# Five seams of a hybrid attention and DeltaNet block reordered, and three of seven weight low parts moved to GpSimd

## What is computed

```
proj = x @ w_in                       # 1024 x 4872, split into the parts below
A = banded_sink_attention(rope(q), rope(k), v)          # 8 heads, window of 128 rows
B = gated_delta_rule(conv+silu(q, k, v), beta, decay)   # 4 heads of 128, chunks of 64 rows
merged = sigmoid(gA) * (A @ w_branch_attn) + sigmoid(gB) * (B @ w_branch_dn)
x = layer_norm(alpha * x + merged @ w_out)              # "x1" in the kernel
h = square(relu(x @ w_up))                              # w_up is 1024 x 4096
out = layer_norm(alpha * x + h @ w_down)                # w_down is 4096 x 1024
```

## Time and profile before

| | us |
|---|---|
| median of 3 runs | 1459.39 |
| lowest and highest | 1458.61, 1459.73 |
| the profiled execution | 1460.73 |
| its span | 1458.6 |
| TensorE busy | 1424.6 |
| VectorE busy | 895.8 |
| ScalarE busy | 525.5 |
| GpSimd busy | 316.9 |
| mean granted TensorE clock | 0.992 |

### The profile page before, as it was taken

One profiled execution on the slowest core, in us unless ns is written; L12 is line 12 of the kernel. 1 busy time (PEld: TensorE's weight loads), 2 busy tenths in 40 slices (PEclk: granted clock), 3 DMA queues, 4 the chain that ended last, 5 costly groups with the idle time before them and its releaser, 6 DMA issues.

```text
span 1458.6 us, 22456 instructions
## 1 busy us (share of the span) xinstructions
PE 1424.6 (98%) x8570; PEld 1174.7 (81%) x8570; DVE 895.8 (61%) x1710; ACT 525.5 (36%) x1182; POOL 316.9 (22%) x341
## 2 busy tenths in 40 slices
PE   7999999999999999999998999999999999999996
PEld 7888887788888888778887888888888788888885
DVE  3655323565656656365617698666664677777778
ACT  3222212333323232252202435555554544444540
POOL 3666534142432424134820000000000000000000
PEclk9999999999999999999999999999999999999998
DMA  7222533423444233133541234333445866555422
GB/s 219 72 87 106 161 120 107 124 83 84 119 109 117 75 100 95 55 115 133 184 187 58 88 130 152 140 145 148 159 159 192 292 214 189 164 169 182 129 65 116
DMA packets 121007, 194.92 MB, mean 134 GB/s; under 512 B 27664, under 2 KB 67664, under 8 KB 118608
## 3 DMA queue, kind: packets, MB, share of 16 engines
q1 hardware_dynamic: 111984, 174.21, 36.6%
q10 hardware_dynamic: 8928, 19.40, 3.5%
HBM read 135.84 MB, written 57.74 MB: 133 GB/s over the span
## 4 chain that ended last, share of the span: by engine, by line
PE 91%; DVE 5%; ACT 1%; SPq 1%; DMA 1%; issue 1%; ACTq 0%; DVEq 0%
PE ps L1807 15%; PE ps L1742 10%; PE ps L1744 10%; PE ps L1743 10%; PE ps L2177 6%; PE ps L2178 6%; PE ps L2179 6%; PE ps L2160 5%; PE ps L2162 5%; PE ps L2161 5%; PE ps L1875 4%; PE ps L1815 2%; PE ps L1956 1%; PE ps L1907 1%; PE ps L1935 1%; PE ps L1946 1%
## 5 line engine op out<-in xcount | busy, mean ns | idle before, releaser
L713 POOL TENSOR_TENSOR ring2l<-raw,ring2h 128x256 fp32r<-128x256 f32 x180 | 176.6, 1012 | 3.6
L2177 PE MATMUL ps<-thi,shi 128*128 128x512 f32 x416 | 162.0, 390 | 0.0
L2179 PE MATMUL ps<-thi,slow 128*128 128x512 f32 x416 | 161.8, 389 | 0.0
L2178 PE MATMUL ps<-tlow,shi 128*128 128x512 f32 x416 | 161.8, 389 | 0.0
L1807 PE MATMUL ps<-xh,ring2h 128*128 128x512 f32 x304 | 122.5, 403 | 0.0
L1807 PE MATMUL ps<-xl,ring2h 128*128 128x512 f32 x304 | 122.3, 402 | 0.0
L1807 PE MATMUL ps<-xh,ring2l 128*128 128x512 f32 x304 | 119.7, 394 | 0.0
L710 POOL CAST ring2h<-raw 128x1024 fp32r<-128x1024 f32 x45 | 48.5, 1079 | 321.0 <-PE ps L1807 177.6
L1742 PE MATMUL ps<-xh,ring2h 128*128 128x512 f32 x288 | 112.2, 390 | 0.0
L1743 PE MATMUL ps<-xl,ring2h 128*128 128x512 f32 x288 | 112.0, 389 | 0.0
L1744 PE MATMUL ps<-xh,ring2l 128*128 128x512 f32 x288 | 112.0, 389 | 0.0
(11 more groups left out here) (348 smaller groups left out, 3236.3 us busy)
## 6 DMA issues: line engine op xcount, KB each, us to landing
raw<-in_wblk SPq DMA_DIRECT2D x55, 512.0 KB, 3.3
sraw<-hpark SPq DMA_DIRECT2D x104, 256.0 KB, 2.8
hpark<-hq SPq DMA_DIRECT2D x16, 1024.0 KB, 4.6
b<-in_wblk SPq DMA_DIRECT2D x64, 256.0 KB, 3.7
wraw<-in_wblk SPq DMA_DIRECT2D x30, 512.0 KB, 3.8
park<-ub ACTq DMA_DIRECT2D x50, 256.0 KB, 2.0
hpark<-hq SPq DMA_DIRECT2D x16, 768.0 KB, 5.0
park<-cout ACTq DMA_DIRECT2D x12, 512.0 KB, 2.6
```

The lines of the kernel that those rows point to most:

```text
L713: ins = pool.tensor_tensor(lo[:, k:k + 2, :], src[:, k:k + 2, :], hi[:, k:k + 2, :].bitcast(F32), ALU.subtract)
L2177: mm(outp, shi[s][:, ts], thi[m][:, :], start=first, stop=False, skip_group_check=True)
L2178: mm(outp, shi[s][:, ts], tlow[m][:, :], start=False, stop=False, skip_group_check=True)
L2179: return mm(outp, slow[s][:, ts], thi[m][:, :], start=False, stop=final, skip_group_check=True)
```

## The change

1. Start: `xT` lies tile by tile, so that a partition's part of a tile is 4 KB in one piece (before, eight pieces of 512 B). `wav` and tile 0 are loaded in four pairs of transfers, each with two of the eight k-slices, and TensorE begins with each pair.
2. First scan step: another list of fill counts, with the same total.
3. Output projection: TensorE's order becomes tiles 4, 5, transposes 0 and 1, tile 6, transposes 2 and 3, tile 7. VectorE and ScalarE are reordered to fit.
4. From up to down: on ScalarE the snapshot of product 5 goes before `down_s(0)` and `down_t(0)`. On SyncE `store_h(14)` goes behind the first down loads and the first eight B11 pieces.
5. Last rows: flush 5, the statistics of tiles 0 to 3, their deviation and `finish(0)` move into the loop over the steps.
6. Of pairs 4 to 15, the low parts 5 to 7 are subtracted on GpSimd, and TensorE waits for them on `w_ready`.

```diff
--- before.py
+++ after.py
@@ -133,7 +133,7 @@
         xh = at("xh", 0, [P, KT, S], F32R)
         xl = at("xl", 32, [P, KT, S], F32R)
-        xraw = at("xraw", 64, [P, KT, S])
+        xraw = at("xraw", 64, [P, NT, KT, P])
         y = at("y", 64, [P, 2 * NH, S])
         cb = [at(f"cb{p}", 96, [P, 3 + S], extra=p * 4128) for p in range(2)]
@@ -319,7 +319,6 @@
         xh_ok = sem("xh_ok")
         xl_ok = sem("xl_ok")
         c_in = sem("c_in")
-        wav_in = sem("wav_in")
         av_mm = sem("av_mm")
         av_out = sem("av_out")
         zero_ok = sem("zero_ok")
@@ -524,9 +523,12 @@
                     sp.wait_ge(yd_ok, t)
                 sp.dma_start(szt[:, :, :], park[B_DZ:B_DZ + N_DZ, :, bass.ds(PAD + t * P, P)].rearrange("b p s -> p b s")).then_inc(bs_in, 16)
-            sp.dma_start(wavraw[:, :, :], A["wav"]).then_inc(wav_in, 16)
-            for t in range(NT):
-                sp.dma_start(xraw[:, :, t * P:(t + 1) * P], A["xT"][:, :, t * P:(t + 1) * P]).then_inc(x_in[t], 16)
+            for i in range(4):
+                ks = slice(2 * i, 2 * i + 2)
+                sp.dma_start(wavraw[:, ks, :], A["wav"][:, ks, :]).then_inc(up_in[i], 16)
+                sp.dma_start(xraw[:, 0, ks, :], A["xT"][:, 0, ks, :]).then_inc(up_in[i], 16)
+            for t in range(1, NT):
+                sp.dma_start(xraw[:, t, :, :], A["xT"][:, t, :, :]).then_inc(x_in[t], 16)
                 if t in (1, 3):
                     load_w(t // 2, t // 2)
             for dst, name in ((cst[:, :], "cst"), (G[:, :, G_MASK:NV], "mask"), (convw[:, :, :], "convw"), (sink[:, :], "sink"),
@@ -641,7 +643,7 @@
                 for n in (2 * q + 4, 2 * q + 5):
                     if n < NF:
                         load_up(n)
-                if q < NP - 1:
+                if q < NP - 2:
                     store_h(q)
             sp.wait_ge(xp_out[0], 16 * 4)
             sp.wait_ge(xp_out[1], 16 * 4)
@@ -652,6 +654,7 @@
             sp.wait_ge(sp_mm, last + U_P4)
             for i in range(8):
                 load_down("B11", i, b11_in[0])
+            store_h(NP - 2)
             sp.wait_ge(sp_mm, last + U_P5)
             for n in range(4, NSR):
                 load_s(n)
@@ -774,6 +777,12 @@
                 elif j == 6:
                     pool.wait_ge(mg_l, 2 * KT)
                 split(n // 2, n % 2, slh[j], sll[j])
+            for q in range(N_STD + 1, NP):
+                sp_ = q - N_STD
+                for i in range(4, 7):
+                    hi, lo, raw_ = wp[q % 2][UPROD[i][0]]
+                    pool.wait_ge(up_hi, 2 * N_STD + 7 * sp_ + i + 1)
+                    pool.tensor_tensor(lo, raw_, hi.bitcast(F32), ALU.subtract).then_inc(w_ready, 1)
@@ -784,8 +793,12 @@
             cp = lambda o_, i_: act.activation(o_, i_, ACT.Copy)
             for t in range(NT):
-                act.wait_ge(x_in[t], 16)
-                cp(xh[:, :, t * P:(t + 1) * P], xraw[:, :, t * P:(t + 1) * P]).then_inc(xh_ok, 1)
+                if t == 0:
+                    for i in range(4):
+                        act.wait_ge(up_in[i], 32)
+                else:
+                    act.wait_ge(x_in[t], 16)
+                cp(xh[:, :, t * P:(t + 1) * P], xraw[:, t, :, :]).then_inc(xh_ok, 1)
                 act.wait_ge(av_mm, t + 1)
                 cp(vtok[:, t, :], ps[4 + t % 2][:, 0:P])
                 cp(ba[:, t, :], ps[4 + t % 2][:, P:AVW]).then_inc(av_out, 1)
@@ -1008,15 +1021,17 @@
                     act.wait_ge(out_used, n + 1)
                     cp(slh[n][:, :, :], raw[b % 2][:, :].rearrange("p (k c) -> p k c", k=KT)).then_inc(up_hi, 1)
                 else:
-                    act.wait_ge(up_in[n % 4], 16 * (n // 4 + (n % 4 > 1)))
+                    act.wait_ge(up_in[n % 4], 32 + 16 * (n // 4 + (n % 4 > 1)))
                     cp(slh[UP_SLOT[n % 4]][:, :, :], wraw[n % 4][:, :, :]).then_inc(up_hi, 1)
             for t in range(4):
                 norm(t)
-            for t in range(4):
-                x1_hi(t)
+            x1_hi(0)
+            x1_hi(1)
             norm(4)
             norm(5)
+            x1_hi(2)
+            x1_hi(3)
             for n in range(4):
                 up_split(n)
@@ -1075,7 +1090,7 @@
                     cp(shi[s][:, :], sraw[s][:, :]).then_inc(sh_ok, 1)
                 else:
                     i = n - N_RUN
-                    act.wait_ge(x_in[i], 48)
+                    act.wait_ge(x_in[i], 48 if i else 32)
                     cp(shi[NSR + i][:, :], sraw[NSR + i][:, :]).then_inc(lsh_ok, 1)
             def down_t(n):
@@ -1125,13 +1140,11 @@
                 snap(q, U_P5, 2, Q_S2)
                 if q < NP - 1:
                     w_his(q + 1, 3, 7)
-                else:
-                    down_s(0)
-                    down_t(0)
                 snap(q, U_P1, 3, Q_S3)
                 if q == NP - 1:
-                    down_s(1)
-                    down_t(1)
+                    for n in range(2):
+                        down_s(n)
+                        down_t(n)
                 for i in range(3):
                     c_relu(q, i)
                 for i, k in enumerate((Q_A12, Q_A22, Q_A21)):
@@ -1185,7 +1198,7 @@
             for t in range(NT):
                 dve.wait_ge(xh_ok, t + 1)
                 sl = slice(t * P, (t + 1) * P)
-                tt(xl[:, :, sl], xraw[:, :, sl], xh[:, :, sl].bitcast(F32), ALU.subtract).then_inc(xl_ok, 1)
+                tt(xl[:, :, sl], xraw[:, t, :, :], xh[:, :, sl].bitcast(F32), ALU.subtract).then_inc(xl_ok, 1)
             dve.wait_ge(c_in, 16 * 7)
@@ -1469,7 +1482,7 @@
             def combine(t):
-                dve.wait_ge(x_in[t], 32)
+                dve.wait_ge(x_in[t], 32 if t else 16)
                 for n in range(2):
                     dve.wait_ge(oz_mm, 2 * t + n + 1)
                     bank = 2 * t + n if t < 4 else 2 * (t % 2) + n
@@ -1512,20 +1525,20 @@
             for t in range(4):
                 place1(t)
             combine(4)
+            combine(5)
             x1_lo(0)
             x1_lo(1)
             stats(4)
-            combine(5)
-            x1_lo(2)
-            x1_lo(3)
             stats(5)
             deviation(4, 6)
             place1(4)
             place1(5)
             combine(6)
-            stats(6)
+            x1_lo(2)
+            x1_lo(3)
             up_lo(0)
             up_lo(1)
+            stats(6)
             combine(7)
             stats(7)
             up_lo(2)
@@ -1579,7 +1592,7 @@
                 w = {k: v[2] for k, v in wp[q % 2].items()}
                 s = q - N_STD
                 for n in (2 * q, 2 * q + 1):
-                    dve.wait_ge(up_in[n % 4], 16 * (n // 4 + (n % 4 > 1)))
+                    dve.wait_ge(up_in[n % 4], 32 + 16 * (n // 4 + (n % 4 > 1)))
                 tt(w["S1"], w["S3"], w["A22"], ALU.add).then_inc(tx_sum, 1)
                 dve.wait_ge(tx_sum, 8 + 4 * s + 1)
                 tt(w["S2"], w["S1"], w["A11"], ALU.subtract).then_inc(tx_sum, 1)
@@ -1591,6 +1604,8 @@
             def w_los(q, first=0, last=7):
                 s = q - N_STD
                 for i in range(first, last):
+                    if q > N_STD and i >= 4:
+                        continue
                     hi, lo, raw_ = wp[q % 2][UPROD[i][0]]
                     dve.wait_ge(up_hi, 2 * N_STD + 7 * s + i + 1)
                     tt(lo, raw_, hi.bitcast(F32), ALU.subtract).then_inc(up_w, 1)
@@ -1702,8 +1717,17 @@
                 for kind in T_ADDS:
                     if T_ADD0[kind] <= n < T_ADD0[kind] + NP:
                         t_add(kind, n - T_ADD0[kind])
-                if j and 4 <= i < 8:
-                    flush(j - 1, i - 4)
+                f = i - (1 if j == 6 else 4)
+                if j and 0 <= f < 4:
+                    flush(j - 1, f)
+                if j == 6 and 0 < f <= 4:
+                    dve.wait_ge(fl_ok, 20 + f)
+                    half_stats(f - 1, 0)
+                if j == 6 and f == 5:
+                    deviation2(0, 4)
+                    dve.wait_ge(gb_in, 32)
+                if j == 6 and f > 5:
+                    finish(f - 6)
                 if 72 <= n < 76:
                     dve.wait_ge(fl_ok, 16)
                     half_stats(n - 72, 1)
@@ -1714,12 +1738,7 @@
                     lo_s(N_RUN + n - LAST_S0)
                 if LAST_T0 <= n < LAST_T0 + N_LAST:
                     lo_t(N_RUN + n - LAST_T0)
-            dve.wait_ge(fl_ok, 24)
-            for t in range(4):
-                half_stats(t, 0)
-            deviation2(0, 4)
-            dve.wait_ge(gb_in, 32)
-            for t in range(4):
+            for t in range(1, 4):
                 finish(t)
             for t in range(4, NT):
                 flush(6, t - 4)
@@ -1744,13 +1763,14 @@
                 return mm(outp, ll, rh, start=False, stop=stop)
             for t in range(NT):
-                if t == 0:
-                    pe.wait_ge(wav_in, 16)
-                pe.wait_ge(x_in[t], 16)
```

(19 more changed lines are left out.)

## The result

The changed kernel takes 1448.68 us (median of four runs, 1447.91 to 1449.76) beside 1459.56 us for the kernel before (four runs, 1458.61 to 1460.22): ratio 0.9926, 95% interval 0.9909 to 0.9944, so 10.9 us faster. The forecast was 1445.9 us, and the time lies inside its range of 1441.2 to 1450.5. The profiled execution took 1447.91 us, with a span of 1446.1; it is the fastest of its four, while the profiled one of before was 1.3 us over its median. Trace against trace the gain is therefore 12.5 us of span, where the sum of the steps was 13.5. Of the 2.8 us between forecast and median, 0.7 lie in the trace (1447.91 beside the 1447.2 of the sum), and 2.1 in that the profiled execution was taken to lie 1.3 us over its median and lay 0.8 under it.

What follows compares the result with a forecast made beforehand. TensorE, busy 98% of the span, was taken as the bound, leaving 34 us of standstill and low-clock work to gain. Gains of 2.4 + 1.2 + 7.5 + 0.9 + 1.5 + 0 = 13.5 us gave 1445.9 us, range 1441.2 to 1450.5.

Steps and rivals of the forecast that it cites:

- Seams 2, 3 and 5: First scan step's fill counts gain 1.2 us, reordered output projection and transposes 7.5, last rows moved forward 1.5.
- seam 3: Output projection and transposes: up(0) starts 7.5 us sooner, 4.1 from waits, 3.1 from half clock, the rest edges; bounds 5 and 7.9.
- Seam 1: Start, xT relaid and first loads in pairs: block 0 at 22.1 instead of 24.5 us, gain 2.4; bounds 0.3 and 3.6.
- the prediction's own sign: Wrong if a wait over 1 us stands at the start, first scan step or output projection, or span moves under 9 us.
- one more pair every 0.85 us: Start: first pair lands near 3.7 us, more every 0.85; then tiles land one per 1.47 us, at 357 GB/s.
- tile 0 counts about double: Start: tile 0 runs slow and counts as two of nine units, 1.87 us a tile; it ends near 7.4 us.
- Seam 4: Up pairs to down products: third down step 3.9 us sooner, new 2.5 us wait before it; net gain 0.9, bounds 0 and 3.9.
- The clock term: Behind the new wait before down step 2 the clock falls, costing 3.0 us.
- rival B: The new 2.5 us wait before down step 2 leaves the clock up: 3.0 us more gained, 1442.9 us; chance 0.26.
- GpSimd's low parts: Three of seven low parts of an up pair on GpSimd: 12 us of slack, gain zero; bounds -0 and +3 us.
- C: Start stays bound by its transfers, as 357 GB/s was seen only in short stretches: 2.1 us less gained, 1448.0; chance 0.14.
- A: The forecast itself, 1445.9 us, with granted clock 0.50 behind the new wait before down step 2; chance 0.50.

Runs made afterwards that it cites:

- the last run: Changed kernel with wav and tile 0 loaded whole, ten zero-tile matmuls ahead, and operands of down steps 2 and 3 made early: 1441.52 us.

## Why the prediction was right and where it was not

- **Seams 2, 3 and 5** came as worked out (1.46, 7.76 and 1.46 us; 1.2, 7.5 and 1.5 forecast), and undoing them brings back 1.56, 6.4 and 1.45. For seam 3 the sizes in the sum (waits plus half clock plus edges) fit the two traces; that the undone one loses 1.0 us less between the same two marks shows that the clock's share of such a price is not fixed.
- **Seam 1** failed, by the prediction's own sign too: it called itself wrong if a wait over 1 us stood in seams 1 to 3, and two do (1.44 and 1.19 us). Two steps of it were wrong. The first is "one more pair every 0.85 us ... From there the tiles are paced by their landing, one per 1.47 us". I priced the tiles by bytes and one rate, and left out when each is issued, how long one is under way, and that pieces of 1 KB move slower. The first pair landed as said, and the rate rose as said (420 GB/s from 14 us on, beside 291 in the earlier trace rows). But from 2 to 6 us it was 258, not 357, and tile 1 was issued 2.8 us later than it could have been and landed 6.0 us after that. The row that says it was there: the first loads landed 6.1 us after their issue. The second is "tile 0 counts about double": it bound the low clock to tile 0, which was to end near 7.4. In the eight traces the clock is low behind the start of tile 1, for 2.0 us of loss on the mean, and with whole loads and no wait at all it rises only at 11.78. The bound of 0.3 us for this seam was too high as well; a loss hadn't been bounded. By the page "DMA: Bandwidth & Descriptors" (Specifications) of the Trainium skill, pieces of 512 B already run at full rate and the layout would give nothing. The runs speak against it: the same tile 0, with wav, is there 4.4 us after its issue in pieces of 4 KB and 6.9 us in pieces of 512 B.
- **Seam 4.** Wait and sooner start were right within 0.1 us: 2.5 and 3.9 us forecast, 2.40 and 3.86 measured. The clock term was mis-sized: 3.0 us taken from longer waits, 1.4 measured. The timeline of the granted clock is at 0.50 for 3.4 us here, for 6.8 us behind the 3.5 us wait of before. And rival B is partly true: in ten traces with this wait (2.2 to 2.9 us), seven show the fall at a cost of 1.4 to 1.6 us, and three (whole loads, zero tile, fill counts and last rows undone; waits of 2.40, 2.45 and 2.23) don't. A window of the changed kernel, at the end of its wait of 2.40 us (the first 0.83 us are still the wait):

```profile
1133.00:1135.00 2.00, 1.18 (x3) 1.01 (x4) 2.00 (x5) 0.86 (x2) 0.00 (x0) 0.61 1.03 421
```

The same window of the run with whole loads, where the wait, of 2.40 us too, ended at 1132.01:

```profile
1133.00:1135.00 2.00, 2.00 (x10) 1.69 (x9) 2.00 (x5) 0.00 (x0) 0.00 (x0) 1.00 0.96 373
```

- **GpSimd's low parts** cost nothing, as said. The page "SBUF — State Buffer" (Who interferes with whom) of the Trainium skill says that the two engines take turns when a VectorE operation has two SBUF inputs and GpSimd reads SBUF. The direction agrees: only VectorE's operations with both inputs in SBUF grew, by 0.17 and 0.38 us on the mean. That is less than a GpSimd instruction of 1.3 us, but waiting for the rest of one that has begun would look the same, so the runs don't tell turns from sharing.
- **Rivals.** C (the start stays bound by its transfers, 1448.0) is nearest to the measured 1448.7, but its reason holds only in part: the later rate did rise, and what was late are the second tile, behind small pieces and late issues, and the clock. Of 3.1 us too much at the start, 1.6 came back at the clock. That two wrong terms had opposite signs is luck: with the forecast 3.0 us at the clock the median would have been near 1450.3, at the edge of the range. A's condition, low clock behind the new wait, came in seven of ten traces, at half of its price.

## What to carry to other kernels

Before you split a first load to start sooner, write down the issue time, the size of the pieces and the landing of the load behind it: here each extra issue costs 0.47 us of queue, and eight small ones moved the next tile's issue by 2.8 us and its landing by 2.4, which left nothing of the early start. When a seam leaves a wait of known size, look at the order of the engine it waits for and of the one that feeds that engine, and whether the next operation is one that nobody is waiting for: here an idle gap of 2.2 us stood right ahead. A wait's price in clock is a range, not a number; take the wait away rather than reckon with it.

## What the hardware showed

- Equal waits don't cost the same clock: 2.36 and 2.40 us fell, 2.40 and 2.45 didn't. The lower clock stood for 3.4 us in the seven cases behind these waits and for 6.8 us behind those of 3.3 and 3.5 us and behind the pair of waits at the transposes.
- Matmuls on a zero tile before the data raise the clock: at 5.98 us with them (6.76 in the last run), at 11.78 us with the same loads without them. That is worth 1.5 us in a kernel of 1440.
- A transfer of 512 KB in pieces of 4 KB lands in 4.4 to 4.7 us at the start of the program (three traces), and in 6 to 12 us when others are queued ahead of it, though SyncE spends about the same on it (0.42 us, and 0.45 to 0.53 us on the median).
- With the DMA engines 0.90 busy from 2 to 6 us, pieces of 1 KB move at 258 GB/s and pieces of 4 KB at 328.
